# Two attention stages of a transformer kernel, re-staged on TensorE: pairs of 64-row heads, one-pass masks, finer lanes, an output product in two halves

## The reference

```python
def stick_breaking_attention(q, k, v):            # layer 0: 16 heads of 64
    z = einsum(q, k) / 8;  earlier = key_pos < q_pos
    log_keep = where(earlier, log_sigmoid(-z), 0)
    log_after = cumsum(log_keep, reverse=True) - log_keep
    weight = where(earlier, exp(log_sigmoid(z) + log_after), 0)
    return einsum(weight, v)
def diff_mixer(h, ...):                            # layer 1: 8 heads, two maps of 64 each
    q, k = rms_norm_2(q, q_g), rms_norm_2(k, k_g)  # over 64 columns
    q1, q2, k1, k2 = partial_rope(...)             # first 16 of 64 columns turned
    a = softmax(mask(q1 k1 / 8)) - lam * softmax(mask(q2 k2 / 8))
    o = rms_norm_2(a @ v, sub_g) * (1 - lam_init)
# each layer: x += mixer(rms_norm(x)) @ w_out ; x += ffn(rms_norm(x))
```

## Time and profile before

| | us |
|---|---|
| median of 3 runs (lowest, highest) | 2463.02 (2460.88, 2464.46) |
| the profiled execution: its time, and its span in the trace | 2461.2, 2459.2 |
| PE busy over the span | 2331.8 (95%) |
| DVE, ACT, POOL busy | 1265.5, 1010.0, 293.8 |
| mean granted clock of TensorE | 0.969 |

### The profile page before, as it was taken

One profiled execution on the slowest core, in us unless ns is written; L12 is line 12 of the kernel. 1 busy time (PEld: TensorE's weight loads), 2 busy tenths in 40 slices (PEclk: granted clock), 3 DMA queues, 4 the chain that ended last, 5 costly groups with the idle time before them and its releaser, 6 DMA issues.

```text
span 2459.2 us, 36108 instructions
## 1 busy us (share of the span) xinstructions
PE 2331.8 (95%) x15048; PEld 1766.2 (72%) x15048; DVE 1265.5 (51%) x2296; ACT 1010.0 (41%) x1993; POOL 293.8 (12%) x361
## 2 busy tenths in 40 slices
PE   6999999999999986999999999999999988999999
PEld 4777777777778864876647888887865546888887
DVE  5677777677444566322227543445445546443442
ACT  4455555555452254445544322333334434322231
POOL 0022221122200032122221000001000001000000
PEclk9999999999999998999979999999999878999999
DMA  4111111111142321111002322322110101222222
GB/s 150 52 57 62 45 61 54 48 62 46 65 143 94 140 74 51 52 52 35 35 18 73 103 103 86 102 88 96 58 69 18 35 18 52 103 94 94 100 89 86
DMA packets 29106, 175.90 MB, mean 72 GB/s; under 512 B 3216, under 2 KB 3600, under 8 KB 9744
## 3 DMA queue, kind: packets, MB, share of 16 engines
q1 hardware_dynamic: 28944, 173.60, 20.4%
HBM read 167.29 MB, written 6.29 MB: 71 GB/s over the span
## 4 chain that ended last, share of the span: by engine, by line
PE 90%; DVE 5%; ACT 2%; issue 1%; DMA 1%; POOL 0%; SPq 0%; DVEq 0%; ACTq 0%
PE ps L1374 89%; PE ps L1377 1%; ACT arena L2284 1%; DMA raw<-wstream 0%; DVE on_t L2119 0%; DVE spl L1802 0%; DVE arena L2097 0%; ACT hh L2287 0%; DVE arena_r L2054 0%; DVE arena L2089 0%; ACT spl L2287 0%; DVE arena L2241 0%; DVE arena L2236 0%; ACT arena L2287 0%; DVE arena L2008 0%
## 5 line engine op out<-in xcount | busy, mean ns | idle before, releaser
L1374 PE MATMUL ps<-hh,spl 128*128 128x512 f32 x3104 | 1048.9, 410 | 24.6 <-DVE hl L2123 11.8
L1374 PEld LDWEIGHTS ps<-hh,spl 128*128 128x128 f32 x3104 | 584.5, 190 | 173.9 <-issue 41.8
L1374 PE MATMUL ps<-hl,spl 128*128 128x512 f32 x1552 | 633.4, 408 | 0.0
L1374 PE MATMUL ps<-arena_r,spl 128*128 128x512 f32 x2064 | 490.0, 398 | 9.9 <-ACT arena_r L2287 6.7
L1802 DVE TENSOR_TENSOR spl<-raw,spl 128x512 fp32r<-128x512 f32 x596 | 412.1, 719 | 137.0 <-ACT spl L2287 136.0
L1374 PEld LDWEIGHTS ps<-arena_r,spl 128*128 128x128 f32 x2064 | 390.1, 189 | 109.5 <-issue 12.1
L2287 ACT ACTIVATE spl<-raw 128x512 fp32r<-128x512 f32 x596 | 342.5, 618 | 154.2 <-PE ps L1374 153.1
L1374 PEld LDWEIGHTS ps<-hl,spl 128*128 128x128 f32 x1552 | 295.7, 191 | 72.3 <-issue 17.0
L1374 PE MATMUL ps<-arena 32*32 32x32 f32 (+6 forms) x5664 | 306.0, 228 | 30.6 <-DVE arena L2241 11.8
L1374 PEld LDWEIGHTS ps<-arena 32*32 32x32 f32 (+3 forms) x5664 | 167.9, 119 | 144.6 <-issue 102.7
L2284 ACT ACTIVATE arena<-arena 128x512 f32<-128x512 f32 (+3 forms) x303 | 170.3, 563 | 208.9 <-DVE arena L2165 141.4
(11 more groups left out here) (213 smaller groups left out, 2070.9 us busy)
## 6 DMA issues: line engine op xcount, KB each, us to landing
raw<-wstream SPq DMA_DIRECT2D x149, 1024.0 KB, 4.9
on_t<-spill SPq DMA_DIRECT2D x10, 256.0 KB, 3.6
x<-xT SPq DMA_DIRECT2D x4, 512.0 KB, 7.1
spill<-x SPq DMA_DIRECT2D x8, 256.0 KB, 2.3
spill<-arena SPq DMA_DIRECT2D x8, 256.0 KB, 2.0
x<-xT SPq DMA_DIRECT2D x1, 2048.0 KB, 7.7
out<-x SPq DMA_DIRECT2D x8, 256.0 KB, 2.0
arena<-spill SPq DMA_DIRECT2D x6, 256.0 KB, 2.9
```

Of the source, the lines that this page charges most:

```text
L1374: return pe.matmul(out, lhsT, rhs, start=start, stop=stop, skip_group_check=True)
```

## The change

In the order of the code:

- `Order.step`: a lane that added nothing last time is no longer asked at once, but only when its time is due. This holds for the whole program, the first block too.
- Layer 0: the two heads of a pair become one step. `st_z` issues two 64-row products one behind the other, into two neighbouring banks (rows 0 to 63 and 64 to 127 of the array); ACT, DVE and POOL take both banks in one instruction of twice the columns. `st_o` issues two products of 64 value columns each, into partitions 0 to 63 and 64 to 127 of one bank. The mask product takes fp32r operands (`ident_r`, `mask_r`), one pass in place of four. The lane is cut in `stick_front` (scores to masked softplus) and `stick_back`, for even and odd pairs each, with three buffers, and each engine's share is a step of its own.
- Layer 1: `df_s` likewise takes both maps in one step, with the one-pass mask; two rope lanes with two sets of tiles; the norm weight is folded into the rotation matrix and the cosines once (four DVE operations in `lambda`), which takes one ACT operation out of `br_in`; `br_rot` comes before `br_ss`; `diff_lane` is cut in `score_lane` and `mix_lane`.
- The output product: `split_lane` splits each tile when it is done (`os_hi` on ACT, `os_lo` on DVE, two operations), there is no drain ahead, and `out_proj` runs eight gemms over blocks 0 to 3 (heads 0 to 7, or 0 to 3 in layer 1), adds them to x, and then eight over blocks 4 to 7. The weights are laid out in that order. This makes 32 additions to x (`xo`) of the 16.

The number of `mul` products (6720) is unchanged.

```diff
-            if lane[0] and (lane[2] or lane[1] <= self.clock["PE"] - self.margin) and self.dry(lane, SLACK):
+            if lane[0] and lane[1] <= self.clock["PE"] - self.margin and self.dry(lane, SLACK):
                 moved = self.advance(lane) or moved
...
+    def split_lane(name, op, k, ready):
+
+        while not all(key in o.at for key in ready):
+            yield
+        o.behind(*[o.at[key] for key in ready])
+        yield "AC"
+        o.add("os_hi", name, k, cost=[("AC", AC_B)])
+        yield "DV"
+        st = o.add("os_lo", name, k, cost=[("DV", DV_B)])
+        op.ready[k], op.t[k] = ("os_lo", st.n), st.t
+
+    def out_proj(op, name):
+
+        def first_done(m):
+            def f(u):
+                st = o.main("xo", name, 0, m, cost=[("DV", DV_B)])
+                st.u, st.m, st.part = u, m, 0
+                main.give(u)
+            return f
+
         def done(m):
             def f(u):
-                st = o.main("xo", name, m, cost=[("DV", DV_B)])
-                st.u, st.m = u, m
+                st = o.main("xo", name, 1, m, cost=[("DV", DV_B)])
+                st.u, st.m, st.part = u, m, 1
                 main.give(u)
                 square(name, m, "x")
                 feed(name, m)
             return f
         for m in range(KT):
-            gemm(op, KT, done(m))
+            gemm(op, 4, first_done(m))
+        for m in range(KT):
+            gemm(op, (4, 5, 6, 7), done(m))
+        o.drain()
         o.flush()
 
...
+    def stick_front(m):
+
         while m not in qk_of:
             yield
-        iqk = qk_of[m]
-        uo = L["o"].take()
-        _, sum_old = L["sum"].take()
+        o.behind(o.at["st_q", m], o.at["st_k", m])
         for kb in (3, 2, 1, 0):
-            n = S - 128 * kb
-            f = n / 512
-            u = L["z"].take()
-            ie, e_old = L["e"].take()
-            isp, sp_old = L["sp"].take()
-            st = o.add("st_z", m, b, kb, cost=[("PE", 0.2 + 0.86 * f), ("AC", 0.2 + 0.42 * f), ("AC", 0.2 + 0.42 * f),
-                                               ("AC", 0.2 + 0.42 * f), ("DV", 0.15 + 0.54 * f), ("PO", 0.56)])
-            st.u, st.iqk, st.isp, st.sp_old, st.e_old = u, iqk, isp, sp_old, e_old
-            L["e"].give(ie, st)
-            yield
-            iw, w_old = L["w"].take()
-            st = o.add("st_w", m, b, kb, cost=[("PE", 0.25 + 0.86 * f + (0.86 * (f - 0.25) if kb < 3 else 0)),
-                                               ("AC", 0.2 + 0.42 * f)])
-            st.u, st.isp, st.iw, st.w_old, st.sum_old = u, isp, iw, w_old, sum_old
...
+            while ("st_p", m, kb) not in o.at or not wt.ready():
                 yield
-            st = o.add("st_o", m, b, kb, cost=[("PE", 0.86 * f)])
+            iw, w_old = wt.take()
+            o.behind(o.at["st_p", m, kb], last, w_old)
+            yield
+            z = o.at["st_z", m, kb]
+            st = o.add("st_w", m, kb, cost=[("PE", 0.25 + 1.72 * f + 1.72 * (f - 0.25)), ("AC", 0.2 + 0.84 * f)])
+            st.u, st.isp, st.iw, st.w_old, st.sum_old = z.u, z.isp, iw, w_old, sum_old
+            pairs.give(z.u)
+            last = st
+            if kb:
+                t = o.now
+                last = o.add("st_su", m, kb, cost=[("PO", 0.8 + 2 * (f - 0.25))])
+                o.now = t
+            last.u, last.isp = z.u, z.isp
+            last.sum_old = sum_old
+            sp.give(z.isp, last)
+            yield
+            while ("v_out", 0, kb, m // 2) not in o.at or not uo and not obs.ready():
+                yield
+            uo = uo or obs.take()
+            st = o.add("st_o", m, kb, cost=[("PE", 0.1 + 0.86 * f)], u=uo)
             st.u, st.iw = uo, iw
-            L["w"].give(iw, st)
-        L["sum"].give(0, o.at["st_w", m, b, 0])
-        st = o.add("st_out", m, b, cost=[("DV", 0.6)])
...
+        o.behind(t_old)
+        st = o.add("br_in", which, m, cost=[("DV", DV_B), ("AC", AC_B)], after=u.t)
+        st.u, st.which, st.old, st.i = u, which, t_old, i
         main.give(u)
         yield
-        while not aux.ready():
...
-            yield
-        st = o.add("br_rot", which, m, cost=[("PE", PE_B), ("DV", DV_B), ("PO", PO_B)])
-        st.u = aux.take()
-        aux.give(st.u)
-        yield
+        while not ring.ready():
+            yield
+        banked("br_rot", which, m, cost=[("PE", PE_B), ("DV", DV_B)]).i = i
+        yield "AC"
+        while not ring.ready():
+            yield "AC"
+        banked("br_ss", which, m, cost=[("PE", PE_B), ("AC", AC_B), ("AC", AC_B)]).i = i
+        yield "DV"
         st = o.add("br_out", which, m, cost=[("DV", DV_B), ("DV", DV_B)])
-        st.which, st.iqk, st.old = which, iqk, old
+        st.which, st.iqk, st.old, st.i = which, iqk, old, i
...
             ip, p_old = pp.take()
-            for j in range(2):
-                while not sbk.ready():
-                    yield
-                st = o.add("df_s", m, qb, j, cost=[("PE", 0.3 + 0.86 * f), ("DV", 0.15 + 0.54 * f), ("AC", 0.25 + 0.42 * f)])
-                st.u, st.iqk, st.ip, st.old = sbk.take(), iqk, ip, p_old
-                sbk.give(st.u)
-                yield
-                o.add("df_r", m, qb, j, cost=[("DV", 0.15 + 0.1 * j)])
-            st = o.add("df_p", m, qb, cost=[("DV", 0.15 + 0.3 * f), ("DV", 0.15 + 0.54 * f)])
-            st.ip = ip
-            yield
-            while not tbk.ready():
-                yield
...
+    def mix_lane(m, qb, ip, iat, at_old, iqk):
+        f = (qb + 1) / 4
+        o.behind(o.at["df_s", m, qb])
+        yield "DV"
+        st = o.add("df_p", m, qb, cost=[("DV", 0.15), ("DV", 0.15), ("DV", 0.15 + 0.3 * f), ("DV", 0.15 + 0.54 * f)])
+        st.ip = ip
+        engine = "AC" if qb % 2 else "DV"
+        yield engine
+        while not ring.ready():
+            yield engine
+        st = banked("df_t", m, qb, cost=[("PE", 0.11 * (qb + 1)), (engine, 0.2 + 0.5 * f)])
+        st.ip, st.iat, st.old = ip, iat, at_old
+        pp.give(ip, st)
+        if qb < 3:
...
+                    w.wait_ge(sem("rope_c"), 1)
+                    ts(cos2, cos2, q2w, None, ALU.mult).then_inc(sem("rope_c"), 1)
+                    ts(rot_of["q"], C["rot_b"], q2w, None, ALU.mult).then_inc(sem("rope_c"), 1)
+                    ts(rot_of["k"], C["rot_b"], V("k2"), None, ALU.mult).then_inc(sem("rope_c"), 1)
...
                         t = at["st_q", m].u
                         w.wait_ge(drained[t.b], t.n)
-                    q_, k_ = (a[r, :] for a in qk_of[q.iqk])
-                    mm(psum[u.b][:, 0:n], k_[:, kb * 128:kb * 128 + 128], q_[:, kb * 128:S], True, False) \
-                        .then_inc(sem(f"st_z{b}"), 1)
+                    q_, k_ = qk_of[q.iqk]
+                    for b in range(2):
+                        r = slice(64 * b, 64 * b + 64)
+                        i = mm(psum[u.b + b][:, 0:n], k_[r, kb * 128:kb * 128 + 128], q_[r, kb * 128:S], True, False)
+                    i.then_inc(sem("st_z"), 1)
...
+                    u, n, sp = q.u, S - 128 * kb, sp_of[q.isp]
+                    if q.n == 1:
+                        w.wait_ge(sem("mask_r"), 2)
+                    w.wait_ge(sem("st_mask"), at["st_p", m, kb].n)
+                    for b in range(2):
+                        mm(psum[u.b + b][:, 0:128], ident_r[:, :], mask_r[:, 0:128], False, False)
+                    for b in range(2):
+                        i = mm(psum[u.b + b][:, 0:n], C["neg_tri_l"], sp[:, b, 0:n], False, kb == 3)
                     if kb < 3:
-                        w.wait_ge(sem(f"st_sum{b}"), 3 * m + 3 - kb)
-                        i = mm(o[:, 128:n], C["neg_ones"], ln[b]["sum"][:, kb * 128 + 128:S], False, True)
...
                         t = at["v_out", 0, kb, m // 2].u
                         w.wait_ge(drained[t.b], t.n)
-                    mm(psum[u.b][:, kb * 128:S], v8[:, kb, m * 128:m * 128 + 128], ln[b]["w"][q.iw][:, 0:n], kb == 3,
-                       kb == 0).then_inc(sem(f"st_o{b}"), 1)
+                    for b in range(2):
+                        c = m * 128 + 64 * b
+                        i = mm(psum[u.b][64 * b:64 * b + 64, kb * 128:S], v8[:, kb, c:c + 64], wt_of[q.iw][:, b, 0:n],
+                               kb == 3, kb == 0)
...
-                        w.wait_ge(sem("br_out"), max(at["br_out", w, m].n for w in "qk"))
-                    q_, k_ = (a[r, :] for a in qk_of[q.iqk])
-                    o = psum[u.b]
-                    mm(o[:, 0:n], q_[:, qb * 128:n], k_[:, 0:n], True, False)
-                    mm(o[:, n - 64:n], C["ident"], C["neg64"][:, 0:64], False, True).then_inc(filled[u.b], 1)
+                    if qb == 0:
+                        w.wait_ge(sem("br_out"), max(at["br_out", c, m].n for c in "qk"))
+                    q_, k_ = qk2_of[q.iqk]
+                    for j in range(2):
+                        r = slice(64 * j, 64 * j + 64)
+                        mm(psum[u.b + j][:, 0:n], q_[r, qb * 128:n], k_[r, 0:n], True, False)
```

(14 more changed lines are left out.)

443 lines of the change are left out of this document (214 added, 229 removed).

## The result

The changed kernel takes 2339.67 us (median of 4 runs, 2338.57 to 2341.43), the kernel before 2462.43 (4 runs): a ratio of 0.950, 95% interval 0.9485 to 0.9518. The forecast was 2327, its own range 2305 to 2342. The profiled execution has a span of 2336.8 us, 122.4 less than before's 2459.2, where the sum had 134.5.

A forecast was written before the change was run, and what follows sets the result against it. TensorE was taken to bound the kernel, through its work and idle time. Gains of 41.6 (layer 0 work), 37.6 (layer 1 work), 20 and 37 (lost time), less 1.5, made 134.5 off 2461.2: 2327 us, own range 2305 to 2342.

The forecast's parts named there:

- (a): Layer 0 scores: two heads' 64-row products run side by side, gaining 3.8 us a head pair.
- (d): Layer 1 scores and masks: paired products and one-pass masks gain 4.7 us a head pair, 37.6 us.
- (b): Layer 0 value products: two 64-column products side by side gain 0.5 us a head pair.
- (c): Masks of layer 0: one pass in place of four, eight a head pair, gains 0.9 us a head pair.
- (e): Tail of layer 0: of 25 us lost, 5 stay, gain 20; bounds nothing or 25.
- The other distance: Sign: the same place in two successive head pairs of layer 0 lies 26 to 27 us apart.
- R1: Rival: column halves of the array do not overlap, costing 17 us, total 2344; 0.14 together with a partial-overlap variant.
- (f): Layer 1's lost time, 62 us: two rope lanes, wider step spacing and no drain leave 25, gain 37.
- R2: Rival: layer 1's lost time stays, bound by a step's chain, not TensorE; total 2374, chance 0.17.
- (g): Extra `xo` additions, wider operations, half gemms and lane rule: priced at zero; first block -5 to +8 us.
- R3: Rival: paired steps make TensorE wait and its clock fall in both stages; 64 us slower, 2525; chance 0.03.
- R4: Rival: 64-row pairs do not overlap beyond 128 columns, so scores gain only shape switches; 2379, chance 0.05.

The follow-up runs named there:

- experiment 1: Changed kernel with both score products of a pair on rows 0 to 63, so not side by side, in both layers: 2380.68 us.
- experiment 2: Changed kernel with layer 0's value products taking all 128 value columns, not two 64-column products side by side: 2347.49 us.
- experiment 4: Changed kernel with all lanes drained again ahead of the output product in both layers: 2368.5 us.
- experiment 5: Changed kernel with a single rope lane and one set of its buffers in layer 1: 2334.26 us.
- experiment 6: Changed kernel, layer 1: rotation's addition on GpSimd with a new order (2329.5 us), in the old order (stage 328.3 us), and the new order alone (2329.65 us).

## Why the prediction was right, and where it was not

It was right in direction, size and mechanism; the sum was 12 us too large. Of these, 7 lie in layer 1, 3 in the FFNs and 2 in the first block. That layer 0 came out at 61.4 where the sum had 61.6 is luck: 5.9 more of work and 6.1 less of lost time cancel.

(a) and (d), pairs: the overlap as priced. Without it the second product of 512 columns costs 0.85 us, and the stages have 16.7 and 16.4 us more work (experiment 1, 17 expected). The changes of shape that went with the pairs (128 to 64 in layer 1) no run took back. The Trainium skill, "TensorE: Matmul & The Clock Gate", Part 3, has matmuls start and end in program order; from it the prediction worked out 1.5 times one product for a four-pass pair, by letting the second product start only behind the first one's first record. That working is what the trace speaks against: a pair took as long as one, for rows and for columns. The order itself may stand, for the pair's records start in twos 7 and 6 ns apart.

(b), column halves: mis-sized at 0.5 a pair; 1.3 by the work of experiment 2. Over eight pairs the difference is 6.4 us, which is about layer 0's 5.9 us of work above the sum. The term had a change of shape into and out of every value pair, and 49 of 64 stood there.

(c), masks: 0.11 a mask holds, and 7 us a layer (6.5 to 8.4 of work in four stages).

(e), tail of layer 0: 13.9 of lost time went in the whole stage, not 20; the missing drain gave 11.4 (experiment 4). The sign that was named for it failed: 86 us from the last projection product to the FFN, not 65 to 70, since more heads' steps now stand behind that product. The work was moved, not lost; a distance between two marks says something only when the same work lies between them. The clock there was 0.96. The other distance held: even and odd pairs have lanes of their own and lie some 18 and 33 us apart in turn, so the same place is two pairs on (scores of 512 columns at 1085.5, 1138.3 and 1189.2; at 1104.5 and 1156.7), 25.5 to 26.4 a pair for the 26 to 27 forecast; 28.7 would have said R1.

(f), lost time of layer 1: 31.2 gained where 35.5 stood; 36.3 us are left where the term had 25, out of 67.5 and not 62. Size nearly right, reason partly wrong: the stage with one rope lane is no longer (experiment 5), the missing drain gave 14.4 (experiment 4). Of the 29 us of idle time left, some 12 came from where the plan put steps (experiment 6), which neither (f) nor R2 had named. R2, with layer 1's stage at 350, falls: 319.0. The Trainium skill's "TensorEngine Tiling (Array Packing)", PSUM Bottleneck, says that packing speeds TensorE and not the emptying of PSUM, which may then become the bottleneck. The trace does not show that here: the row maxima that empty the packed scores' banks are in none of TensorE's waits of the stage. The emptying of a projection bank is in them, with 7.2 us (`br_in`, L2276), and that bank is not a packed one.

(g), the edits at nothing: right for the wider operations, wrong for the feed. A half gemm of 2.8 us no longer covers the 3.2 us that DVE takes for a tile; both FFNs start squeezed and lose 1.6 us, the last three gemms of the output product 1.9 more. That is some 3.5 us a layer which the sum had at nothing. The first block's +2.1 was within its bounds; as it varies by 10 us between runs here, it can't be called an effect of the lane rule. That rule was not tried alone, nor were the folded norm weights and the new order of `br_rot` and `br_ss`.

R3 and R4 fall with the clock (0.97 in both stages) and with the pairs. Waits on ACT and DVE did not grow in layer 0: TensorE's idle time there went from 16.8 to 13.7 us.

## What to carry to other kernels

When a gemm is cut in halves, work out what each in-order engine must do per half, not per gemm: the feed of the next stage had 5.5 us to hide under and now has 2.8. An experiment that moves an operation in a planned program also moves the plan; hold the order fixed, or run the order alone, before the operation gets the credit. And read a stage as idle, half clock and work apart: idle time and work repeated within about 1 us between kernels of one order, the length only within some 4.
